# Depthwise convolution of the odd channel tiles moved to ScalarE and GpSimd, and the conv norm's steps moved up by one tile

## The reference, cut to what matters

```python
u = z[..., OFF_CA:OFF_CB] * jax.nn.sigmoid(z[..., OFF_CB:OFF_GM])
padded = jnp.concatenate([conv_buf.astype(u.dtype), u], axis=1)
cv = depthwise_conv_valid(padded, conv_w, conv_b)      # 31 taps, each channel by itself, + bias
cv = jax.nn.silu(layernorm(cv, ln_g, ln_b))            # over the 1024 channels of a frame
branch_c = cv @ w_branch_c.astype(cv.dtype)
merged = gm * branch_m + gc * branch_c                 # gm, gc: sigmoids of two parts of z
```

## Time and profile before

| | us |
|---|---|
| median of 3 runs | 1241.97 (1241.71 to 1244.38) |
| the profiled execution, its own time | 1242.71 |
| its span, first to last instruction | 1241.0 |
| TensorE busy | 1203.5 (97%) |
| VectorE busy | 862.0 (69%) |
| ScalarE busy | 452.0 (36%) |
| GpSimd busy | 21.8 (2%) |

### The profile page before, as it was taken

One profiled execution on the slowest core, in us unless ns is written; L12 is line 12 of the kernel. 1 busy time (PEld: TensorE's weight loads), 2 busy tenths in 40 slices (PEclk: granted clock), 3 DMA queues, 4 the chain that ended last, 5 costly groups with the idle time before them and its releaser, 6 DMA issues.

```text
span 1241.0 us, 19863 instructions
## 1 busy us (share of the span) xinstructions
PE 1203.5 (97%) x7536; PEld 1124.0 (91%) x7536; DVE 862.0 (69%) x1542; ACT 452.0 (36%) x671; POOL 21.8 (2%) x37
## 2 busy tenths in 40 slices
PE   8999999999999999899999999979999999999987
PEld 7998999899899989799999898878998989989886
DVE  5633469878987989788654454986676666666667
ACT  5442243124323422311246323443535335253352
POOL 2000000000000000200000000000000000000000
PEclk9999999999999999999999999989999999999999
DMA  8342352344226322332322226122213231332232
GB/s 236 109 108 85 100 153 69 102 122 113 68 85 169 82 76 80 105 88 69 86 68 69 68 69 237 68 89 98 101 53 119 69 119 50 104 119 78 93 131 90
DMA packets 147844, 124.05 MB, mean 100 GB/s; under 512 B 13615, under 2 KB 131591, under 8 KB 147762
## 3 DMA queue, kind: packets, MB, share of 16 engines
q1 hardware_dynamic: 125138, 99.03, 27.1%
q10 hardware_dynamic: 22624, 23.95, 5.9%
HBM read 106.13 MB, written 16.83 MB: 99 GB/s over the span
## 4 chain that ended last, share of the span: by engine, by line
PE 87%; DVE 5%; ACT 3%; issue 3%; DMA 1%; SPq 0%; ACTq 0%; DVEq 0%; POOLq 0%; POOL 0%
PE out L416 42%; PE out L2309 15%; PE bank L2348 10%; PE out L2348 6%; PE bank L1997 6%; PE bank L1992 3%; PE out L2259 2%; PE bank L2259 2%; DVE WK L1251 1%; DVE WK L1248 1%; DVE CV L1251 1%; DMA WK<-in_x_prompt 1%; PE out L397 1%; ACT GH L733 1%; ACT CV L733 1%
## 5 line engine op out<-in xcount | busy, mean ns | idle before, releaser
L416 PE MATMUL out<-XH,WH 128*128 128x328 f32 (+1 forms) x1024 | 241.7, 317 | 0.8 <-DVE WL L345 0.7
L416 PE MATMUL out<-XH,WL 128*128 128x328 f32 (+1 forms) x1024 | 239.4, 315 | 0.0
L416 PE MATMUL out<-XL,WH 128*128 128x328 f32 (+1 forms) x1024 | 239.0, 315 | 0.0
L1251 DVE SCALAR_TENSOR_TENSOR CV<-WK,cwu,CV 128x512 f32 (+1 forms) x480 | 226.5, 546 | 0.0
L416 PEld LDWEIGHTS out<-XH,WH 128*128 128x128 f32 x1024 | 172.6, 189 | 5.2 <-issue 4.7
L416 PEld LDWEIGHTS out<-XH,WL 128*128 128x128 f32 x1024 | 173.4, 189 | 3.3 <-issue 3.1
L416 PEld LDWEIGHTS out<-XL,WH 128*128 128x128 f32 x1024 | 173.5, 189 | 3.0 <-issue 2.8
L345 DVE TENSOR_TENSOR WL<-ST,WH 128x1024 fp32r<-128x1024 f32 x85 | 104.5, 1229 | 86.4 <-ACT WH L337 75.0
L337 ACT ACTIVATE WH<-ST 128x1024 fp32r<-128x1024 f32 x85 | 89.7, 1056 | 96.8 <-PE out L416 46.3
L767 ACT ACTIVATE WK<-out 128x656 f32<-128x656 f32 (+1 forms) x56 | 40.1, 716 | 211.9 <-PE out L416 210.5
L1248 DVE TENSOR_TENSOR WK<-out,WK 128x512 f32<-128x512 f32 (+3 forms) x82 | 44.8, 570 | 53.8 <-PE out L416 32.0
(11 more groups left out here) (252 smaller groups left out, 2141.9 us busy)
## 6 DMA issues: line engine op xcount, KB each, us to landing
ST<-in_w_in SPq DMA_DIRECT2D x65, 512.0 KB, 4.1
ST<-in_w_ff SPq DMA_DIRECT2D x32, 1024.0 KB, 5.3
WK<-in_state_mlstm_C ACTq DMA_DIRECT2D x32, 256.0 KB, 3.6
o_C_sample<-WK ACTq DMA_DIRECT2D x32, 256.0 KB, 2.5
WK<-in_x_prompt SPq DMA_DIRECT2D x8, 512.0 KB, 7.3
ST<-in_w_branch_m SPq DMA_DIRECT2D x8, 512.0 KB, 4.5
ST<-in_w_branch_c SPq DMA_DIRECT2D x8, 512.0 KB, 4.1
ST<-in_w_out SPq DMA_DIRECT2D x8, 512.0 KB, 3.6
```

Source lines behind the costliest of these rows:

```text
L416: last = pe.matmul(out[s][:, h, 0:H], w[:, s, kk, :], x[:, kk, h * H:(h + 1) * H], start=(m < 2), stop=(m >= len(ms) - 2))
L1251: return dve.scalar_tensor_tensor(o, x, s, y, op0, op1)
```

## The change

- `CONV_TILE`, `CONV_SLOT`: VectorE keeps the even channel tile of each head, 31 taps, all behind tiles n + 2 to n + 7 (5, 3, 6, 6, 6, 5). In the slots it has none.
- The odd channel tile of each head: ScalarE multiplies (`odd_products`), two instructions a tap; product 0 goes with the bias into `CV`, the others into a ring of 4 buffers of 128x640. GpSimd adds each of the 30 buffers to `CV` (`odd_adds`). Three products stand behind each of tiles n + 2 to n + 7, 2 each in slots 0, 1, 7, 8, 9, 10, and one in slot 11. In the gates, 3 stand behind tiles 4 and 5, 6 behind the high half of tile 8, and so on (3 after each sigmoid, 6 after a pair of branch tiles).
- A product waits for the add that frees its buffer (`conv_odd`), an add for its product (`tap`) and the add before it. The conversion of the next input tile and SyncE's reload of the cache columns wait for the odd adds too.
- ScalarE's loop over heads is written out, as the ring's places differ for the last head.
- The conv norm's steps stand one tile earlier: the last adds of the sum at the end of gates tile 15, all others at r - 1.

```diff
-CONV_TILE = {2: 7, 3: 4, 4: 7, 5: 7, 6: 7, 7: 3}
-CONV_SLOT = {0: 3, 2: 3, 3: 3, 4: 2, 5: 3, 6: 2, 7: 3, 8: 3, 9: 3, 10: 2}
-TAPS = 2 * CONV_W
+CONV_TILE = {2: 5, 3: 3, 4: 6, 5: 6, 6: 6, 7: 5}
+TAPS = CONV_W
+ODD_TILE = {2: 3, 3: 3, 4: 3, 5: 3, 6: 3, 7: 3}
+ODD_SLOT = {0: 2, 1: 2, 7: 2, 8: 2, 9: 2, 10: 2, 11: 1}
+TRING = 4
...
 # SyncE, before the cache columns of the last head
             sp.wait_ge(sem("conv"), 2 * TAPS * 3)
+            sp.wait_ge(sem("conv_odd"), (TAPS - 1) * 3)
...
 # GpSimd
+            def odd_adds(u):
+                kk = 2 * u + 1
+                for t in range(1, TAPS):
+                    g.wait_ge(sem("tap"), TAPS * u + t + 1)
+                    wait(g, "conv_odd", (TAPS - 1) * u + t - 1)
+                    g.tensor_tensor(CV[:, kk, :], CV[:, kk, :], tapped[u // 3][t % TRING], ALU.add
+                                    ).then_inc(sem("conv_odd"), 1)
+            for u in range(HEADS - 1):
+                odd_adds(u)
...
 # ScalarE
+            def odd_products(u, t0, count):
+                kk = 2 * u + 1
+                for t in range(t0, min(t0 + count, TAPS)):
+                    if t == 0:
+                        evacuated(act, N(N_HEADS0 + PER_HEAD - 1, PER_HEAD, u))
+                        act.wait_ge(sem("cache_in"), 32 * (u + 1))
+                        wait(act, "conv_odd", (TAPS - 1) * u)
+                    elif t > TRING:
+                        act.wait_ge(sem("conv_odd"), (TAPS - 1) * u + t - TRING)
+                    to = tapped[u // 3][t % TRING] if t else CV[:, kk, :]
+                    fn, kw = (ACT.Copy, {}) if t else (ACT.Identity, dict(bias=vec("conv_b", kk)))
+                    act.activation(to[:, 0:TS].rearrange("p (b t) -> p b t", b=NB), ups[:, 1, :, t:t + LB], fn,
+                                   scale=cwt[:, kk, t:t + 1], **kw)
+                    copy(to[:, TS:T2], up[:, 1, NMETA + t:NMETA + t + SEQ], "tap", fn, scale=cwt[:, kk, t:t + 1], **kw)
...
-            head(0)
-            with act.Fori(1, HEADS) as i:
+            for i in range(HEADS):
                 head(i)
...
 # VectorE, at the end of gates tile 15 (was at r == 0 of the next loop)
+                if j == 2 * KT - 1:
+                    dve.wait_ge(sem("conv"), 2 * TAPS * HEADS)
+                    dve.wait_ge(sem("conv_odd"), (TAPS - 1) * HEADS)
+                    dve.wait_ge(sem("csum"), KT - 3)
+                    V.link(tt(ln[0], ln[0], CV[:, KT - 2, :], ALU.add))
+                    tt(ln[0], ln[0], CV[:, KT - 1, :], ALU.add).then_inc(sem("lsum"), 1)
```

More of the change, by code:

```diff
@@ L78 @@
 V_HEAD = 26
[L81 to L84 removed]
+CONV_TILE = {2: 5, 3: 3, 4: 6, 5: 6, 6: 6, 7: 5}
[3 more added lines that the diff above has]
+TRING = 4
+assert sum(ODD_TILE.values()) + sum(ODD_SLOT.values()) == TAPS
+assert sum(CONV_TILE.values()) == TAPS
 def build(nc, a):
@@ L206, in build @@
     x2q = wk(10 * D + 2 * T2, D)
+    tapped = [[over(f"tapped{at}_{o}", [T2], F32, at, o)[:, :] for j, (at, o) in enumerate(places)] for places in (
+        ((at_gh, 6 * T2), (at_gh, 7 * T2), (at_gl, 6 * T2), (at_gl, 7 * T2)),
+        ((at_wk, off["vt"] + 2), (at_wk, off["vt"] + 2 + T2), (at_wk, off["so"] + 2), (at_wk, off["so"] + 2 + T2)))]
     mis = sb("mis", [P, 16])
@@ L900, in head @@
                 n = N(N_HEADS0, PER_HEAD, i)
-                first = isinstance(i, int)
+                first, t = i == 0, 0
                 hi(n + 1)
@@ L915, in head @@
                 evac(n + 2, two(q[:, 0, :]))
+                if not first:
+                    t = odd_products(i - 1, t, ODD_TILE[2])
                 hi(n + 4)
@@ L925, in head @@
                 c0t_copy(i, 0)
+                if not first:
+                    t = odd_products(i - 1, t, ODD_TILE[3])
                 hi(n + 5)
@@ L931, in head @@
                 c0t_copy(i, 1)
+                if not first:
+                    t = odd_products(i - 1, t, ODD_TILE[4])
                 hi(n + 6)
@@ L938, in head @@
                 c0t_copy(i, 2)
+                if not first:
+                    t = odd_products(i - 1, t, ODD_TILE[5])
                 hi(n + 7)
@@ L947, in head @@
                 c0t_copy(i, 3)
+                if not first:
+                    t = odd_products(i - 1, t, ODD_TILE[6])
                 hi(n + 8)
                 evac(n + 7, two(so[:, 1, :]), ACT.Sigmoid)
+                if not first:
+                    t = odd_products(i - 1, t, ODD_TILE[7])
                 if first:
@@ L968, in head @@
                         c0t_copy(i, TR_SLOT[s])
+                    if not first and s in ODD_SLOT:
+                        t = odd_products(i - 1, t, ODD_SLOT[s])
                     for g in range(C0RING):
@@ L1006, in gates_m @@
                         u_rows(HEADS - 1)
-            gates_m(0)
-            gates_m(1)
+                    else:
+                        t = odd_products(HEADS - 1, t, 6)
+                return t
+            assert gates_m(1, gates_m(0, 0)) == TAPS
+            act.wait_ge(sem("conv_odd"), (TAPS - 1) * HEADS)
+            act.wait_ge(sem("np_out"), 16 * HEADS)
             for b in range(C0RING):
@@ L1016, in _ @@
                 hi(N(N_GC0 + r + 1))
-                if r == 5:
+                if r == 4:
                     act.wait_ge(sem("t_lr"), 1)
@@ L1025, in _ @@
                         copy(ln[2 + kk % 2], CV[:, kk, :], "csq", ACT.Square)
-                if r >= 6:
-                    for kk in range(4 * (r - 6), 4 * (r - 5)):
+                if r in (5, 6):
+                    for kk in range(4 * (r - 5), 4 * (r - 4)):
                         act.wait_ge(sem("cvn"), kk + 1)
@@ L1491, in conv_input @@
                 evacuated(dve, n + (r - 1))
-                wait(dve, "conv", 2 * TAPS * (i - 1) + (TAPS if x == 0 else 2 * TAPS))
+                wait(dve, "conv_odd" if x else "conv", (TAPS - 1 if x else 2 * TAPS) * i)
                 wait(dve, "t_u", i)
@@ L1633, in _ @@
                 lo(N(N_GC0 + r + 1))
[L1634 to L1639, removed]
+                if r == 1:
                     dve.wait_ge(sem("mean"), 2)
```

48 lines of the change are left out of this document (25 added, 23 removed).

## The result

| | before | after |
|---|---|---|
| median of the runs | 1241.84 us (4 runs) | 1316.87 us (4 runs, 1314.39 to 1321.49) |
| ratio | | 1.0605, 95% interval 1.0579 to 1.0631 |
| span of the profiled execution | 1241.0 | 1312.3 |

What follows compares the result with a forecast made beforehand. TensorE sets the time, with VectorE close behind and a lead of 3.1 us at the first scores. Heads 52.9 plus gates 10.2 make 63.1 us on the median 1241.97, so 1305 us; range 1262 to 1326.

Steps and rivals of the forecast that it cites:

- TensorE bound, nothing to win: Second head: TensorE works 114.86 of 116.10 us, so hardly anything to win; the question is whether VectorE keeps its lead.
- The price of an add: Beside GpSimd's adds: each add costs VectorE 1.2 us, with bounds of 1.0 and 1.41.
- The sum over the head's tile part: Heads 1 to 3: VectorE's work ends at 350.8, first scores 16.5 us late; with clock loss 52.9 us over three heads.
- the 8 us forecast at slot 1: Each head, slot 1: TensorE waits some 8 us for the scores, a sign that would show the forecast right.
- TensorE's waits end on ScalarE: A sign that would show the forecast wrong: TensorE's waits trace back to ScalarE; no size given.
- Rival C: Heads: ScalarE becomes the bound through the ring of 4, adds sitting out two VectorE instructions; 1315 to 1330 us, chance 0.10.
- The clock: After a head's last wait: half-clock stretch losing 1.7 us a head, hidden inside the tile part; one existing stretch replaced.
- three products ahead of a high half: Heads, tile part: ScalarE's products delay a weight's high half by 2.9 us, hidden in the tile of 7.22.
- the adds of slots 7 to 11: End of each head: 9 adds, 11 us of VectorE, where 27 taps or 25 us went; cost nothing.
- Gates: Head 3's convolution in the gates: splits 6, 7, 8 late, together 8.5 us, plus a 1.7 clock stretch: 10.2.
- Conv norm: Norm steps one tile earlier: the one wait of 2.2 us moves, same size; 0, between -2.2 and +2.2.

Runs made afterwards that it cites:

- e11: The changed kernel with ScalarE's products 1 to 30 and GpSimd's adds cut to one column, all waits and order kept: 1244.5 us, ratio 1.0013.
- e1: The changed kernel with GpSimd's adds cut to one column of 640, ScalarE's products, waits and order kept: 1258.8 us, ratio 1.0122.
- e2: The changed kernel with each GpSimd add replaced by a copy of the product buffer to CV, 640 columns: 1264.2 us, ratio 1.0166.
- e4: The changed kernel with GpSimd's adds cut to columns 0 to 319: 1263.5 us, ratio 1.0160.
- e3: The changed kernel with products 1 to 30 cut to one column and GpSimd adding CV to itself at full size: 1286.2 us, ratio 1.0343.
- e5: The changed kernel with 14 of the 31 even taps moved to slots 2 to 6, nothing left out: 1285.9 us, ratio 1.0343.
- e10: The changed kernel with adds of one column and no products in slots 0 and 1: 1248.1 us, ratio 1.0046.
- e8: The changed kernel with the four products of slots 0 and 1 moved into tiles n + 3 to n + 6: 1306.3 us, ratio 1.0507.
- e6: The kernel before the change with only the conv norm's steps one tile earlier: 1243.6 us, ratio 1.0005.

## Why the prediction was right, and where it was short

**TensorE bound, nothing to win.** Held. With both new operations shrunk and VectorE's taps halved (e11) the kernel is no faster than before.

**The mechanism, and luck in the number.** The mechanism held: an add on GpSimd holds VectorE, VectorE is late with the low halves, and TensorE waits. The total is near for a poorer reason, as two terms missed in opposite ways:

| | waits: forecast | measured | busy TensorE (clock): forecast | measured |
|---|---|---|---|---|
| heads 1 to 3 | 49.5 | 35.2 | 3.4 | 22.2 |
| gates and the first tile | 8.5 | 7.3 | 1.7 | 4.8 |

The waits are those of TensorE's idle time, after less before; for the gates before that is 115.5 us with 112.3 busy. In the sum the waits were put 15.5 us too high and the clock 21.9 too low. With the 2.0 us behind the gates, put at 0, this makes 71.5 for 63.1.

**The price of an add.** 1.2 us was taken from small instructions beside five adds; 1.31 was measured in the rounds. e1, e2 and e4 move the size and the time follows. The Trainium skill (SBUF — State Buffer, "Who interferes with whom") says that the two exclude each other. The traces agree that one stands while the other has its turn, but not on a price of the whole instruction: an add with no VectorE beside it took 1.57 to 1.59 us here and held VectorE for 1.31; for the add of e3 it was 1.25 and 1.00, for that of e4 0.87 and 1.03, for the copy of e2 0.72 and 0.78. That the page's price put the forecast at 1314, near the result, is therefore no proof of it. Neither rule nor row told that an add may instead stand for 6 us. And I counted taps and splits as held because they read two SBUF operands. Of the three delayed instructions in the earlier trace rows the tensor_scalar reads one, and was held for 1.01; so was the scaling of the changed kernel.

**The sum over the head's tile part.** What it counts is right: VectorE's order, not its load, and e5 shows it from the other side, with 14 taps less ahead of the scores and 31 us back. The waits came where they were put, at the weights of the tile part and ahead of slot 1, in head 2 1.15, 2.64, 1.41 and 2.08 us by the weights and 2.9 by the scores. Of the 8 us forecast at slot 1 head 2 showed 2.9, since the five taps of tile n + 7 ran undisturbed in 4.70 us while an add stood. In heads 1 and 3 this turned round: TensorE waited 4.7 us for ScalarE. That TensorE's waits end on ScalarE was one of my signs of being wrong, and for 9.4 of the 39 us of waits in the heads they do. Rival C had the ring as the bound, but by adds that sit out two instructions, not ten, and it shows at one place only, not in each tile.

**The clock, the term that was mis-sized.** I put it at one stretch of 1.7 us a head, counted only behind the last wait and hidden in the tile part. Measured were 10.5, 2.5 and 9.2. Behind slot 1 the clock was mostly at the lower of its two levels for 10 us (changed kernel, columns as above):

```profile
236.00:248.00 12.00, 9.82 (x32) 7.91 (x33) 4.20 (x9) 1.09 (x2) 5.30 (x4) 0.57 0.18 44
366.00:377.00 11.00, 8.10 (x44) 6.25 (x42) 8.19 (x15) 2.42 (x5) 10.43 (x5) 0.63 0.19 50
```

In the first of them TensorE was busy for 9.82 of the 12 us; 9.82 x (1 - 0.57) = 4.2 us is an estimate of what full clock would have saved. In head 1 the lower clock began already behind the wait of 4.7 us at slot 0 (0.51 from 229.2 to 234.2), and a shorter stretch followed the wait of 2.66 in the tile part (0.74 from 204.2 to 209.2), where I had taken it as hidden.

**Slot 1, a wait that was left out.** I wrote that three products ahead of a high half are hidden in the tile, and did not follow the five of tile n + 7 and slot 0 to the one high half with no tile to hide in: that of tile n + 9, which VectorE splits ahead of the four updates that TensorE waits for. There was no lead to spend at this step: in the earlier trace rows TensorE waits 0.5 us there. In the change it waits 3.2 and 3.1 us in heads 1 and 3. Moving the four products of slots 0 and 1 away gave 10.7 us (e1 to e10) and 10.5 (the change to e8). Most of that is busy time at the lower clock and not the wait. No run shows apart whether this wait is what brings the lower clock. Nor can the figure be added to the 63 forecast: the three heads as a whole came out at 57.4 for 52.9.

**End of the head.** I took the adds of slots 7 to 11 as free. They were not quite: the last add of the head ended at 285.9, and the conversion of the next input tile, which waits for it, made the first split of the next head late, 1.9 and 1.6 us. Between conversion and split lie 5 us in which VectorE waited for nothing that the profile shows; the kernel before has them too.

**Gates.** 10.2 forecast, 12.1 measured; the waits at tiles 7 and 8 were 5.0 and 2.3, in place of 2.4 and 5.5.

**Conv norm.** 0 forecast; e6 measured 1.0005. In place of 2.2 and 0.7 us there is one of 3.4.

**Open.** Why an add gets in between two taps in one round and stands through ten in another was not settled. The rounds differ in when the add asks, but no run moved that alone.

## What to carry to other kernels

An engine with time to spare is no help if its instructions hold another's: before moving element-wise work from VectorE to GpSimd, look which VectorE instructions beside it would be held (here taps, splits and a tensor_scalar out of SBUF, not the updates out of PSUM), and pay each GpSimd instruction out of the lead at the place where the next engine waits. Price TensorE's waits with the lower clock behind them: in the heads it cost 22 us beside 35 of waits. Moving work also means reading on, past the tile, to the first instruction behind it in that engine's order which someone waits for. And a step shifted earlier gained nothing by itself; shifted and with the short work that has a deadline put ahead of the long one, it gained 0.5%.

## What the runs showed of the hardware that was not expected

- An add on GpSimd (128x640) that asked while VectorE ran taps one behind the other stood for 5.88 and 6.30 us, 7.51 at most, while others with the same neighbours took about 2. Alone it took 1.57 to 1.59.
- The hold on VectorE is 1.31 us for an add of two different tiles, 1.00 for one of a tile with itself, 1.03 for one of 320 columns, 0.78 for a copy. Adds of one column added 0.01 to a round.
- A tensor_scalar that reads one tensor from SBUF is held as well: 1.65 us for 0.34 beside an add, and 1.18 for 0.17. Four updates out of PSUM were not, 2.72 with and without full adds beside them.
- The lower clock can outweigh the waits: e8 waited 6.2 us more than the change and was faster by 9.1 us in the profiled executions, as TensorE was busy for 15.3 us less.
- After waits of 4.7 and 3.2 us close together the granted clock was 0.57 over the next 12 us, where a single wait of 2.2 us was followed by 3.5 us at 0.53.
